# A two-block transformer on one core: the layer stages joined by token tile

## What is computed

```python
for l in range(2):
    mod = silu(c) @ ada_w[l] + ada_b[l]      # nine vectors: sh, sc, ga for each step
    h = h + 0.5 * ga1 * swiglu(modulate(rms_norm(h, g0), sh1, sc1), w_in0, w_out0)   # FFN, 2816 wide
    h = h + ga2 * token_mixing(modulate(rms_norm(h, g1), sh2, sc2), ...)
    h = h + 0.5 * ga3 * swiglu(modulate(rms_norm(h, g2), sh3, sc3), w_in1, w_out1)
return rms_norm(h, g_final)
```

## Time and profile before

| | us |
|---|---|
| median of 3 runs | 2194.92 |
| lowest, highest | 2194.91, 2197.24 |
| the profiled execution, its own time | 2195.1 |
| its span | 2193.3 |

### The profile page before, as it was taken

The page is one execution under the profiler, slowest core; times in us unless marked ns, Lnnn a source line. Parts: engine busy times, 40 slices in busy tenths (PEclk is TensorE's granted clock), DMA queues, the critical chain, the costliest instruction groups (busy, mean ns, idle before and its releaser), DMA issues.

```text
span 2193.3 us, 29766 instructions
## 1 busy us (share of the span) xinstructions
PE 1976.0 (90%) x12626; PEld 1758.1 (80%) x12626; DVE 1392.9 (64%) x1456; ACT 998.4 (46%) x1150; POOL 89.2 (4%) x105
## 2 busy tenths in 40 slices
PE   7888789999996999897996899989998979888997
PEld 3876678888885999896775789979997977667997
DVE  4878458999995777554335667767755443455445
ACT  4354347777774333433444433343334433534343
POOL 0220100000001000000000000000001000000000
PEclk9999869999997999997998999989999989989999
DMA  8655418999983777452312377737753432223553
GB/s 344 225 203 203 173 66 335 375 351 349 351 339 152 288 295 281 173 212 96 116 64 91 144 293 296 280 140 308 294 203 125 183 115 78 77 87 129 188 192 144
DMA packets 63877, 458.42 MB, mean 209 GB/s; under 512 B 7040, under 2 KB 7296, under 8 KB 8832
## 3 DMA queue, kind: packets, MB, share of 16 engines
q1 hardware_dynamic: 63744, 456.51, 55.0%
HBM read 455.43 MB, written 1.05 MB: 208 GB/s over the span
## 4 chain that ended last, share of the span: by engine, by line
issue 41%; PE 38%; DVE 10%; ACT 5%; DMA 3%; POOL 1%; DVEq 1%; POOLq 1%; SPq 0%; ACTq 0%
PE PS L352 11%; PE PS L354 10%; PE PS L353 10%; DVE wlo L279 4%; ACT whi L273 3%; DMA ada<-in_ada 2%; DVE acc L325 2%; PE PS L1110 1%; DMA raw<-in_stream 1%; PE PS L1764 1%; PE PS L338 1%; POOLq L405 1%; POOL st L406 1%; PE PS L1785 1%; PE PS L1773 1%
## 5 line engine op out<-in xcount | busy, mean ns | idle before, releaser
L279 DVE TENSOR_TENSOR wlo<-raw,whi 128x2048 fp32r<-128x2048 f32 x285 | 653.6, 2294 | 500.3 <-ACT whi L273 500.2
L273 ACT ACTIVATE whi<-raw 128x2048 fp32r<-128x2048 f32 x285 | 545.1, 1914 | 509.9 <-PE PS L354 470.7
L352 PE MATMUL PS<-whi,hhi 128*128 128x256 f32 (+1 forms) x1360 | 452.4, 333 | 21.8 <-DVE hlo L475 8.9
L353 PE MATMUL PS<-wlo,hhi 128*128 128x256 f32 (+1 forms) x1360 | 442.5, 325 | 0.0
L354 PE MATMUL PS<-whi,hlo 128*128 128x256 f32 (+1 forms) x1360 | 442.4, 325 | 0.0
L352 PE MATMUL PS<-hhi,whi 128*128 128x256 f32 x1408 | 402.9, 286 | 8.8 <-DVE mod L347 7.1
L353 PE MATMUL PS<-hlo,whi 128*128 128x256 f32 x1408 | 401.0, 285 | 0.0
L354 PE MATMUL PS<-hhi,wlo 128*128 128x256 f32 x1408 | 401.0, 285 | 0.0
L352 PEld LDWEIGHTS PS<-whi,hhi 128*128 128x128 f32 x1360 | 267.2, 196 | 45.5 <-DVE hlo L475 10.4
L352 PEld LDWEIGHTS PS<-hhi,whi 128*128 128x128 f32 x1408 | 273.1, 194 | 12.7 <-DVE mod L347 8.4
L354 PEld LDWEIGHTS PS<-whi,hlo 128*128 128x128 f32 x1360 | 266.3, 196 | 19.4
(11 more groups left out here) (362 smaller groups left out, 1853.5 us busy)
## 6 DMA issues: line engine op xcount, KB each, us to landing
raw<-in_stream SPq DMA_DIRECT2D x285, 1024.0 KB, 4.9
ada<-in_ada SPq DMA_DIRECT2D x92, 1024.0 KB, 4.9
ada<-in_stream SPq DMA_DIRECT2D x48, 1024.0 KB, 4.9
raw<-in_ada SPq DMA_DIRECT2D x3, 1024.0 KB, 15.5
xs<-in_x SPq DMA_DIRECT2D x1, 1024.0 KB, 11.5
Z<-in_ada SPq DMA_DIRECT2D x1, 1024.0 KB, 19.5
Z<-in_ctx SPq DMA_DIRECT2D x1, 1024.0 KB, 10.8
masks<-in_masks SPq DMA_DIRECT2D x2, 512.0 KB, 11.2
```

Of the source, the lines that this page charges most:

```text
L273: nc.scalar.activation(whi[:, s], src, ACT.Copy).then_inc(hi_ready, 1)
L279: nc.vector.tensor_tensor(wlo[:, s], src, whi[:, s].bitcast(F32), ALU.subtract).then_inc(lo_ready, 1)
L352: nc.tensor.matmul(out_, ah, bh, start=start, stop=False, skip_group_check=check)
L353: nc.tensor.matmul(out_, ah, bl, start=False, stop=False, skip_group_check=check)
```

## The change

- **Last three units by tile.** In an FFN the down units of groups 8, 9 and 10 come last (`last_downs`), all for tile 0, then all for tile 1; the weight stream is reordered to match, so groups 9 and 10 have no down unit between them. In `out_product` units 1 to 3 go the same way. Before the third unit of tile 1 stands `between`, the transposes of tile 0 for the next norm.
- **Norm by tile.** `residual`, square, scale, transposes and spread are done for tile 0, then for tile 1. The scale of tile 0 moves to DVE, that of tile 1 to ACT. A spread has 128 tokens: ACT applies scale and shift to blocks 0 to 3 and DVE to 4 to 7, ACT copies out the high parts, DVE subtracts. The conversions of the next stage's first three units stand between these steps on both engines (`norm_act`, `norm_dve`).
- **Next head by tile.** The first three units of the next stage are used for tile 0, with the transposes of tile 1 after the second, and then for tile 1. For a mixer they are three projections. For an FFN they are gate 0, up 0 and gate 1, and groups 0 and 1 (`HEAD`) are computed with the tokens stationary, so that their hidden values stand tokens on partitions and are turned on PE (`head_turn`, 4 transposes each).
- **Gate row** (`gate_pe`, `gate_act`, `gate_pool`) moves behind the head; in the first block behind the routing counts.
- **DVE's order in FFNs.** From group 8 on, the first four half steps stand behind `dve_h`, not ahead of it. In group 1 two conversions stand ahead of `dve_lo`.
- **The end.** The final norm is done by tile; the conversions of the padding units behind the last FFN go. Behind the experts, the conversions of layer 0's second and third unit move behind the squares on ACT and between the two scalings on DVE.

The start of the first block keeps the old norm under new names. The diff, cut to its core:

```diff
         def at_gate(c0, g):
-            return c0 + (3 * g - 1 if g else 0)
+            return c0 + (3 * g - 1 if g else 0) - (g == FFN_GROUPS - 1)
...
+        def last_downs(pe, c0, E0, h0, between):
             for t in range(NT):
+                for g in range(TAIL, FFN_GROUPS):
+                    pe.wait_ge(hlo_done, h0 + (g + 1))
+                    u = unit(pe, at_down(c0, g), E0)
+                    for kk in range(2):
+                        ins = rows_product(u, kk, hid_hi[:, hid(g), kk], hid_lo[:, hid(g), kk], 4, False, False, True, (t,))
+                    if t:
+                        ins.then_inc(unit_used, 1)
+                    if t and g == FFN_GROUPS - 2:
+                        between()
...
+        def hidden_pe(pe, c0, E0, h0, halves, k, l, between):
             v0, nh = halves
+            for t in range(NT):
+                head_part(pe, 0, 0, c0, E0, (t,), lo_at(k, l))
+                head_part(pe, 0, 1, c0, E0, (t,))
+                if t == 0:
+                    norm_pe(pe, N2, k, l, 1, xn, TB)
+                head_part(pe, 1, 0, c0, E0, (t,))
+            gate_pe(pe, N2, k, l, 6)
+            head_turn(pe, 0, h0)
+            head_part(pe, 1, 1, c0, E0, range(NT))
+            if nh:
+                half_sum(pe, v0, 1)
+            pe.wait_ge(*N2.row.at(k, l))
             clear_sums(pe)
+            pe_down(pe, 0, c0, E0, h0)
+            for g in range(2, FFN_GROUPS):
+                sums = g <= nh
                 if sums:
+                    pe.wait_ge(*ada_out.at(v0 + g - 2 - PE_HALVES))
...
+                gate_up(pe, g, 0, c0, E0)
+                if g == 2:
+                    head_turn(pe, 1, h0)
+                gate_up(pe, g, 1, c0, E0)
                 if sums:
                     pe.wait_ge(h_made, h0 + g)
+                    half_sum(pe, v0 + g - 1, 2 * (1 - g % 2) + 1)
+                if g <= TAIL:
+                    pe_down(pe, g - 1, c0, E0, h0)
+            last_downs(pe, c0, E0, h0, between)
...
         def hidden_dve(dve, c0, E0, h0, halves):
...
-                if steps:
+                if steps and g < TAIL:
                     half_steps(dve, v0 + g, 0)
                 dve_h(dve, g, h0)
+                if sums and g == 1:
+                    half_out(dve, v0, 1)
+                if steps and g >= TAIL:
+                    half_steps(dve, v0 + g, 0)
+                if g < TAIL:
+                    conv_lo(dve, c + 1 + RING, E0)
+                if g == 1:
+                    conv_lo(dve, c + 2 + RING, E0)
                 dve_lo(dve, g, h0)
+                if sums and g > 1:
+                    half_out(dve, v0 + g - 1, 2 * (1 - g % 2) + 1)
                 if steps:
                     half_steps(dve, v0 + g, 1)
...
+        def norm_act(act, N, k, l, shift, c, e, x_at):
+            square_act(act, N, k, l, 0, xs, xn, x_at[0])
+            conv_hi(act, c, e)
+            spread_act(act, N, k, l, 0, hhi, shift, TB, am)
+            conv_hi(act, c + 1, e)
+            conv_hi(act, c + 2, e)
+            square_act(act, N, k, l, 1, xs, xn, x_at[1])
+            scale_act(act, N, k, l, xs, xn)
+            spread_act(act, N, k, l, 1, hhi, shift, TB, am)
+        def norm_dve(dve, N, k, l, shift, c, e, y_at):
+            residual(dve, N.x_new, 0, y_at[0])
+            scale_dve(dve, N, k, l, xs, xn)
+            conv_lo(dve, c, e)
+            spread_dve(dve, N, k, l, 0, hhi, hlo, shift, TB, am)
+            residual(dve, N.x_new, 1, y_at[1])
+            conv_lo(dve, c + 1, e)
+            dve.wait_ge(*N.rstd.at(2 * k + 1, l))
+            conv_lo(dve, c + 2, e)
+            spread_dve(dve, N, k, l, 1, hhi, hlo, shift, TB, am)
```

More of the change, by code:

```diff
@@ L374, in rows_product @@
             return ins
[L377 removed]
+        TB = ((2, 3), (4, 5))
         class Norm:
@@ L384, in __init__ @@
                     return
-                self.xa, self.xd, self.am, self.full = (sig(f"{name}_{n}", per) for n in ("scaled0", "scaled1", "factors", "full"))
+                self.scaled = [sig(f"{name}_scaled{t}", per) for t in range(NT)]
+                self.fullB = sig(f"{name}_full", 2 * per)
+                self.am = sig(f"{name}_factors", per)
                 self.turned, self.hi, self.lo = (sig(f"{name}_{n}", 4 * per) for n in ("turned", "hi", "lo"))
@@ L420, in turn @@
                     ins.then_inc(*done.up)
[L422 to L431, removed]
-            act.wait_ge(*N.am.at(k, l))
[L434 to L444, removed]
@@ new lines, in head_part, with head_turn @@
+        def head_part(pe, g, j, c0, E0, tiles, lo_at=None):
+            ins = project(unit(pe, at_gate(c0, g) + j, E0), hhi, hlo, 2 * g + j, tiles, lo_at)
+            if tiles[-1]:
+                ins.then_inc(unit_used, 1)
+        def head_turn(pe, g, h0):
+            pe.wait_ge(h_made, h0 + (g + 1))
+            for c in range(2):
+                for t in range(NT):
+                    ins = nc.tensor.transpose(PS[:, 2 * g, c * 256 + t * P:c * 256 + (t + 1) * P],
+                                              hf[:, g, t, c * P:(c + 1) * P], ident)
+            ins.then_inc(*h_turned.up)
@@ L966, in moe_act @@
             moe_part_act(act, MOE_TILES - 1)
-            for c in range(LAYER0 - 2, LAYER0):
-                conv_hi(act, c + RING)
         def moe_lo_dve(dve, n):
@@ new lines, in norm_dve, with first_norm_act @@
+        def norm_dve(dve, N, k, l, shift, c, e, y_at):
[8 more added lines that the diff above has]
+            spread_dve(dve, N, k, l, 1, hhi, hlo, shift, TB, am)
+        def first_norm_act(act, k, src, dst):
+            for t in range(NT):
+                nc.scalar.activation(dst[:, t], src[:, t], ACT.Square, scale=D ** -0.5,
+                                     accum_out=st[:, t:t + 1]).then_inc(*N1.ss.up)
+                if t == 0:
+                    act.wait_ge(*N1.rstd.at(2 * k))
+                    nc.scalar.activation(dst[:, 0], src[:, 0], ACT.Copy, scale=st[:, 4:5]).then_inc(*N1.scaled[0].up)
@@ new lines, in first_norm_dve, with first_turn @@
+        def first_norm_dve(dve, k, src, dst):
+            dve.wait_ge(*N1.rstd.at(2 * k + 1))
+            nc.vector.tensor_scalar(dst[:, 1], src[:, 1], st[:, 5:6], None, ALU.mult).then_inc(*N1.scaled[1].up)
+        def first_turn(pe, k, src, bank):
+            for t in range(NT):
+                pe.wait_ge(*N1.scaled[t].at(k))
+                for c in range(DC):
+                    o = (c % 2) * 256 + t * P
+                    ins = nc.tensor.transpose(PS[:, bank + c // 2, o:o + P], src[:, t, c * P:(c + 1) * P], ident)
+                    if t and c % 2:
+                        ins.then_inc(*N1.turned.up)
@@ L2301, in hidden_order @@
     seq = [gate[0], up[0]]
-    for g in range(1, n):
+    for g in range(1, n - 2):
         seq += [gate[g], up[g], down[g - 1]]
-    return seq + [down[n - 1]]
+    for g in range(n - 2, n):
+        seq += [gate[g], up[g]]
+    return seq + down[n - 3:]
 def halves(w):
```

443 lines of the change are left out of this document (251 added, 192 removed).

## The result

The changed kernel takes 2182.3 us (median of 4 runs, 2180.4 to 2185.9); the kernel before, run beside it, 2196.1 (2194.9 to 2197.5). The ratio is 0.9943, with a 95% interval of 0.9927 to 0.9959: faster by 0.6%, over the bound of 0.2%. The prediction said 2184. In the profiled executions it is 2195.1 against 2180.4, 14.7 us less where the sum had 11.2.

The account below looks back on a forecast made before the run. PE, busy 90% of the span, was taken as the bound, with time won only in its waits and half-clock stretches. Terms 29.5 - 1.8 + 2.6 + 3 - 13.4 - 8.7 = 11.2 us, off 2195.1, gave 2184, range 2162 to 2199.

Parts of the forecast that it names:

- five joins: Joins between stages of the two layers: cost falls from 76.5 to 47.0 us, a gain of 29.5 us.
- tail of layer 1's FFNs: Last ring unit converted late in layer 1's two FFNs: PE waits about 0.9 us in each, -1.8 us.
- end: Final norm: without padding conversions and with scaling by tile, the last scaling starts earlier, a gain of 2.6 us.
- first mixer to experts: First block's join to the experts: 17.0 us falls to some 13; gain 3, bounds 0 and 5.
- experts to layer 0: Join behind the experts: PE starts about 5 us earlier but at half clock with added work; 0, bounds -3 and +3.
- I take 2.0, since the wait is nearer to the 3.3: At each of the five joins: clock lost behind PE's 2.6 us wait for the second unit's low part, bounds 0 and 2.5.
- (a): Group 9, layer 0's FFNs: PE waits 4.2 us before gate 10 for DVE, plus clock 2.5; twice, -13.4 us.
- (b): Head of three FFNs: late half steps delay loads; PE waits 4.6 us before gate 3, plus clock 2.5; net -8.7 us.
- The halves covered: Rival: DVE and SP run some 4 us ahead at both halves' places, 22 us not lost: 2162; chance 0.16.
- Transposes pull the clock down: Rival: ten groups of 8 transposes in the joins each leave 1.5 us of clock behind: 2199; chance 0.12.
- DVE does not catch up: Rival: groups 2 to 4 of three FFNs, the head's wait returns in the next group, 21 us more: 2205; chance 0.13.
- Joins gain half: Rival: tile 0's chain meets a POOL operation of 2.15 us, not 0.19, at all five joins: 2194; chance 0.09.

Follow-up runs that it names:

- e9b: Changed kernel with the low part of the second head unit written in two passes at the joins, PE starting on the first: 2171.0 us.
- e4: Changed kernel with DVE making the low part of the second head unit ahead of tile 1's residual at the joins: 2187.9 us.
- e5: Changed kernel with the turning of tile 0 behind the last unit of tile 1 instead of ahead of it: 2187.2 us.
- e8: Changed kernel with the order of e2 and e1, and in groups 8 and 9 `half_out` ahead of silu and multiply: 2150.6 us.
- e1: Changed kernel with the first four half steps of groups 8 and 9 moved behind the low part and `half_out`: 2179.9 us.
- e2: Changed kernel with the second four steps of half 1 moved, in group 1, ahead of DVE's two ring conversions: 2156.7 us.
- e12: Changed kernel with only SP's queue altered: at group 2 the two unit loads go ahead of the two loads of half 2: 2174.6 us.
- e11: The kernel before the change, with the same edit as e2 alone: 2194.3 us, ratio 0.9992.
- e6: Changed kernel with 40 more transposes ahead of tile 1's eight, 48 in a row: 2212.2 us.
- e10b: Changed kernel with the edits of e8 and e9b together: 2139.4 us.
- e7: Changed kernel with DVE no longer waiting for POOL between the second unit's low part and the third's: 2185.3 us.

## Why the prediction was right

The terms, from the profiled executions, in us gained:

| term | predicted | measured |
|---|---|---|
| five joins | 76.5 to 47.0: 29.5 | 75.9 to 40.7: 35.2 |
| tail of layer 1's FFNs | -1.8 | -1.7 |
| end | 2.6 | 2.5 |
| first mixer to experts | 3 | 3.2 |
| experts to layer 0 | 0 (-3 to 3) | -1.0 |
| halves, group 9 | -13.4 | -12.5 |
| halves, head | -8.7 | -8.6 |
| not named | | -2.4 |
| sum | 11.2 | 14.7 |

The sum is off by 3.5 us, the joins by 5.7: the other terms are within 1, and the 2.4 that no term named took the rest back, by chance.

**The joins.** The 76.5 held an estimate, 0.6 us for a hole in each first unit; in the trace of the kernel before the holes are 0.55, 0.64, none, 0.55 and 0.70, so the five joins cost 75.9. The 40.7 are first waits 2.2 (3.8 predicted), waits on `wlo` 11.1 (13.0), clock 5.4 (10.0), transposes and gate rows 5 x (0.86 + 0.80 + 1.95) = 18.1 (17.5) and turnings 4.0 (2.7). The mis-sized term is the clock behind the wait on `wlo`: the step "I take 2.0, since the wait is nearer to the 3.3" was too much, it is 0 to 1.6, mean 1.1. The wait itself was named to 0.4 us. That DVE's chain ends it, as the step had it, is shown by e9b; e4 and e5 show that it is that chain's length and not its order that counts. The 7 us at half clock in each join did become 3.6 at the full clock.

**The tail, the end.** The tail's waits are 0.83 and 0.84 for 0.9. That is closer than the working earned: its terms, 6.7 against 5.4 us, give 1.3. At the end the last scaling starts 5.3 us behind the end of the last product, where it was 7.8; POOL's second operation takes 0.54 there:

```profile
2173.63 0.54 POOL L413 TENSOR_TENSOR st<-st,k 128x1 f32<-128x1 f32 x1
```

```profile
2174.29 1.28 DVE L1739 SCALAR_TENSOR_TENSOR Z<-xs,st,Z 128x1024 f32<-128x1024 f32 x1 [2.25 <-POOL st L413]
```

**The first block.** The router's product starts 3.2 us earlier (281.1 for 284.2), layer 0's first FFN 8.1 earlier (692.7 for 700.8). Of the further 4.9, its head gives back 4.1 for tile 1's transposes, gate row and turning, and 1.9 because its first products run at half clock (20 slow products to 697.3, none before the change). These two starts also differ from kernel to kernel by 2 and more, so the terms are not as sure as the figures look. What makes them vary was not followed, but for the load in e8.

**The halves.** (a) Both waits of 4.05 us for the predicted 4.2, the clock 2.2 for 2.5. The mechanism holds in part only: of the 4.05 the steps are 2.0 (e1); the rest is silu, multiply and split, which `half_out` does not need at all (e8). (b) Three waits of 6.66, 4.43 and 4.53 for 4.6 each, and the clock 1.9 each for 2.5; the prediction was 2 us short at one, and the clock made up for it. That one is layer 0's first: there the late steps start 2.6 us behind the turning where it is 1.9 in the other two, and ACT begins on the ring unit 8.4 us behind SP's first unit load where it is 6.8 and 6.9. The order in DVE is the cause (e2) and SP's queue its way to PE (e12). The price of the waits before, 12.6, came out at 12.6 as well; that it had the same root did not (e11).

**The 2.4 not named** lie spread over six stages, -0.4 to 1 us in each, after the waits, the slow products and the added work above are taken off. The trace shows candidates, such as 0.22 us between the last product and the first of eight transposes at 909.14, but they were not counted out.

**The rivals.** The halves covered: no, 23.7 us of waits on `mod`. Transposes pull the clock down: no. Eight at a time they left it at 1.00 at every join, 48 in a row did, and behind an idle stretch the clock rose while PE did nothing else (e6). The rule of the Trainium skill ("TensorE: Matmul & The Clock Gate", Part 4: PE-mode transpose), that transposes don't count as PE-busy in the same way for the clock gate, is not borne out for the f32 transposes of this kernel; the slow ones in the earlier trace rows stood behind an idle stretch. DVE does not catch up: no, the waits stay before gate 3. Joins gain half: no, POOL's operations took 0.19 and 0.54 on tile 0's chain. That the gain survived at all was the joins' doing: the halves took back 21 us of it, and e10b shows that with the halves' steps in the right places and one pass cut in two, the changed kernel stands 57 us under the one before.

## What to carry to other kernels

Before work is moved so that an engine no longer covers a small chore (here the sum of a half), list what stands ahead of that chore in each queue that feeds it: a few lines moved in DVE's order (e8) were worth 32 us, more than twice what the change won. A wait that only moves when the order of two passes is turned belongs to the total of that engine; shortening the pass that ends it helps where turning the order does not. And price a wait on PE with the clock behind it: a split that halves a wait of 2.2 us wins as much again in clock.

## What the runs showed of the hardware

The clock behind a wait does not grow with it. 1.16 us left it at 1.00 (five of five in e9b), 2.2 us cost 0 once and 1.2 to 1.6 four times, 4 to 6.7 us cost 1.1 to 2.4; in e12 a wait of 1.61 us cost nothing, 2.88 and 3.04 us cost 1.5 each. Nor does the length settle it: waits of 2.62 us ahead of tile 1's transposes left it at 1.00 in four of five (e4), with a wait of 1.0 and 3.1 us of products before them. A single stretch varies by over 1 us between kernels with the same wait: behind the 4.53 us in layer 1 the changed kernel lost 1.1, e1_group9 2.3 behind 4.77. What does settle it stays open.

The clock rises under f32 transposes of 128 x 128 alone: 0.50, then 1.00 in one row of them behind a wait of 7.94 us (e6).

A POOL operation on 128 x 1 takes 0.54 us beside an idle DVE and 2.41 beside a DVE conversion (e7). The other of the two operations took 2.15 beside a conversion in the earlier trace rows and takes 0.19 at the joins.
